# One-hots of an expert-weight stage: from two engines to three

## The reference

```python
s = jnp.einsum('nhpd,hpkd->nhpk', q, subkeys)          # q = x_n @ w_q
sv, si = lax.top_k(s, 16)                              # best 16 of 128 keys, twice
cs, cp = lax.top_k(sums of all pairs, 16)              # best 16 of 256 pairs
e = the chosen experts' numbers;  g = softmax(cs)
act = gelu(jnp.einsum('nd,nhkd->nhk', xt, u_tab[e]))
out = jnp.einsum('nhk,nhkd->nd', g * act, v_tab[e])
```

## Time and profile before

| what | value |
|---|---|
| time, median of 3 runs | 2606.37 us (2605.88 to 2607.01) |
| the profiled execution, its time | 2604.28 us |
| its span, first to last instruction | 2602.4 us |
| TensorE, VectorE, ScalarE, GpSimd busy | 92%, 48%, 44%, 31% of the span |
| mean granted TensorE clock | 0.968 of full speed |
| weights and other data read | 338.65 MB, 131 GB/s over the span |

### The profile page before, as it was taken

One profiled execution on the slowest core, in us unless ns is written; L12 is line 12 of the kernel. 1 busy time (PEld: TensorE's weight loads), 2 busy tenths in 40 slices (PEclk: granted clock), 3 DMA queues, 4 the chain that ended last, 5 costly groups with the idle time before them and its releaser, 6 DMA issues.

```text
span 2602.4 us, 47827 instructions
## 1 busy us (share of the span) xinstructions
PE 2392.1 (92%) x16250; PEld 2219.0 (85%) x16250; DVE 1259.4 (48%) x3541; ACT 1142.8 (44%) x2431; POOL 802.9 (31%) x608
## 2 busy tenths in 40 slices
PE   7989999998669999998899989999999668999998
PEld 5789999998559999996674479999999657999997
DVE  5229980002995555553152124992000896555555
ACT  3345444454444444442252235444454444444443
POOL 0067988775000000000000036988878000000000
PEclk9999999999889999998999899999999988999999
DMA  3343444443004444443224433444444002444443
GB/s 137 124 154 121 155 158 164 161 161 113 1 1 161 162 168 163 167 163 129 71 82 134 142 135 133 155 154 158 162 162 161 25 1 83 168 162 168 161 168 108
DMA packets 107490, 341.93 MB, mean 131 GB/s; under 512 B 12466, under 2 KB 30610, under 8 KB 106514
## 3 DMA queue, kind: packets, MB, share of 16 engines
q1 hardware_dynamic: 103968, 333.76, 37.1%
q10 hardware_dynamic: 3442, 7.19, 0.8%
HBM read 338.65 MB, written 1.66 MB: 131 GB/s over the span
## 4 chain that ended last, share of the span: by engine, by line
PE 42%; DVE 7%; POOL 2%; issue 2%; ACT 1%; ACTq 0%; POOLq 0%; DVEq 0%
PE ps L468 16%; PE ps L397 5%; PE ps L399 5%; PE ps L398 5%; DVE ohj L1062 3%; PE ps L371 2%; POOL lo L1293 2%; PE ps L593 2%; DVE HB L1069 2%; PE ps L618 1%; PE ps L522 1%; DVE ohi L1061 1%; PE ps L565 1%; PE ps L546 1%; PE ps L547 1%
## 5 line engine op out<-in xcount | busy, mean ns | idle before, releaser
L1293 POOL TENSOR_TENSOR lo<-raw,hi 128x512 fp32r<-128x512 f32 x576 | 798.4, 1394 | 525.7 <-ACT hi L685 525.2
L685 ACT ACTIVATE hi<-raw 128x512 fp32r<-128x512 f32 x1088 | 655.1, 625 | 483.2 <-PE ps L399 483.1
L397 PE MATMUL ps<-XH,hi 128*128 128x288 f32 x2304 | 687.2, 298 | 35.7 <-POOL lo L1293 18.7
L398 PE MATMUL ps<-XL,hi 128*128 128x288 f32 x2304 | 681.6, 296 | 0.0
L399 PE MATMUL ps<-XH,lo 128*128 128x288 f32 x2304 | 679.3, 295 | 0.0
L468 PE MATMUL ps<-WH,hi 128*128 128x288 f32 x2048 | 605.4, 296 | 6.5 <-DVE lo L1088 6.5
L468 PE MATMUL ps<-WH,lo 128*128 128x288 f32 x2048 | 606.0, 296 | 0.0
L468 PE MATMUL ps<-WL,hi 128*128 128x288 f32 x2048 | 605.4, 296 | 0.0
L397 PEld LDWEIGHTS ps<-XH,hi 128*128 128x128 f32 x2304 | 433.5, 188 | 42.1 <-POOL lo L1293 24.4
L399 PEld LDWEIGHTS ps<-XH,lo 128*128 128x128 f32 x2304 | 435.8, 189 | 0.0
L398 PEld LDWEIGHTS ps<-XL,hi 128*128 128x128 f32 x2304 | 434.6, 189 | 0.1
(11 more groups left out here) (218 smaller groups left out, 1900.8 us busy)
## 6 DMA issues: line engine op xcount, KB each, us to landing
raw<-in_stream SPq DMA_DIRECT2D x592, 512.0 KB, 3.2
pkeys<-in_pool SPq DMA_DIRECT2D x64, 192.0 KB, 3.1
plat<-in_pool SPq DMA_DIRECT2D x64, 128.0 KB, 2.2
SK<-in_sk ACTq DMA_DIRECT2D x2, 1024.0 KB, 6.8
X<-in_x SPq DMA_DIRECT2D x1, 1152.0 KB, 5.6
out_y<-X SPq DMA_DIRECT2D x1, 1152.0 KB, 4.2
wg<-in_wg ACTq DMA_DIRECT2D x1, 1024.0 KB, 10.5
wuk<-in_wuk ACTq DMA_DIRECT2D x1, 1024.0 KB
```

The source lines that it names most:

```text
L397: pe.matmul(ps[s][:, 0:TOK], h, XH[:, c, :], start=c == 0, stop=False)
L398: pe.matmul(ps[s][:, 0:TOK], h, XL[:, c, :], start=False, stop=False)
L685: act.activation(hi[k % 4][:], raw[s][:, half * HALF:(half + 1) * HALF], ACT.Copy)\
L1293: pool.tensor_tensor(lo[k % 4][:], raw[k // 2][:, half], hi[k % 4][:].bitcast(F32), ALU.subtract)\
```

## The change

In the expert-weight stage GpSimd makes all `ohi`, by the same compare that VectorE used. The `ohj` alternate: VectorE makes those of even groups, as before, and ScalarE those of odd groups, as relu(GT - GT (column - JT)²): four squares into a buffer of their own (`DJ`, two of them), then four relus, each with a per-partition scale (`NGT`, the negated weight) and bias (`GT`). The squares of an odd group are made one odd group ahead. VectorE's even one-hots run four groups ahead of the product instead of two. VectorE prepares two small arrays (`NJT`, `NGT`) in place of one (`NIT`). GpSimd waits for the weights and for the last matmul of the first half before it starts; TensorE waits for one semaphore of each one-hot.

```diff
-        NIT = at("NIT", HL + 2048, [P, TOK])
+        NJT = at("NJT", HL + 2048, [P, TOK])
+        NGT = at("NGT", HL + 2048 + TOK, [P, TOK])
+        DJ = [at(f"DJ{b}", HL + 2048 + 2 * TOK + 512 * b, [P, 4, P]) for b in range(2)]
@@ tensor
                 for g in range(NGRP):
                     n = NGRP * l + g
-                    pe.wait_ge(oh_ready, n + 1)
-                    if g % 2:
-                        pe.wait_ge(ohi_ready, NACT * l + g // 2 + 1)
-
+                    pe.wait_ge(ohi_ready, n + 1)
+                    pe.wait_ge((ohj_dve, ohj_act)[g % 2], NACT * l + g // 2 + 1)
@@ scalar
-                act.wait_ge(nit_ready, l + 1)
+                act.wait_ge(ng_ready, l + 1)
+
+                def square_of_difference(k):
+                    if k >= 2:
+                        act.wait_ge(ohj_act, NACT * l + k - 1)
+                    for t in range(4):
+                        n = 4 * (2 * k + 1) + t
+                        ins = act.activation(DJ[k % 2][:, t, :], iota[:], ACT.Square, bias=NJT[:, n:n + 1])
+                    ins.then_inc(dif_sq, 1)
+
+                square_of_difference(0)
                 for k in range(NACT):
                     g = 2 * k + 1
+                    if k + 1 < NACT:
+                        square_of_difference(k + 1)
                     if NGRP * l + g >= 4:
                         act.wait_ge(g_done, NGRP * l + g - 3)
+                    act.wait_ge(dif_sq, NACT * l + k + 1)
                     for t in range(4):
                         n = 4 * g + t
-                        ins = act.activation(ohi[g % 4][:, t, :], iota[:], ACT.Square, bias=NIT[:, n:n + 1])
-                    ins.then_inc(dif_sq, 1)
-                    act.wait_ge(dif_sq, NACT * l + k + 1)
-                    act.activation(ohi[g % 4][:], ohi[g % 4][:], ACT.Relu, scale=-1.0, bias=1.0).then_inc(ohi_ready, 1)
+                        ins = act.activation(ohj[g % 4][:, t, :], DJ[k % 2][:, t, :], ACT.Relu,
+                                             scale=NGT[:, n:n + 1], bias=GT[:, n:n + 1])
+                    ins.then_inc(ohj_act, 1)
@@ vector
-                dve.tensor_scalar(NIT[:], IT[:], -1.0, None, ALU.mult).then_inc(nit_ready, 1)
+                dve.tensor_scalar(NJT[:], JT[:], -1.0, None, ALU.mult)
+                dve.tensor_scalar(NGT[:], GT[:], -1.0, None, ALU.mult).then_inc(ng_ready, 1)
 
                 def g_onehot(g):
                     if NGRP * l + g >= 4:
                         dve.wait_ge(g_done, NGRP * l + g - 3)
                     for t in range(4):
                         n = 4 * g + t
-                        if g % 2 == 0:
-                            dve.tensor_scalar(ohi[g % 4][:, t, :], iota[:], IT[:, n:n + 1], None, ALU.is_equal)
                         ins = dve.tensor_scalar(ohj[g % 4][:, t, :], iota[:], JT[:, n:n + 1], GT[:, n:n + 1],
                                                 ALU.is_equal, ALU.mult)
-                    ins.then_inc(oh_ready, 1)
+                    ins.then_inc(ohj_dve, 1)
...
                 g_onehot(0)
-                g_onehot(1)
+                g_onehot(2)
                 for g in range(NGRP):
-                    if g + 2 < NGRP:
-                        g_onehot(g + 2)
+                    if g % 2 == 0 and g + 4 < NGRP:
+                        g_onehot(g + 4)
                     g_apply(g)
@@ gpsimd
+                pool.wait_ge(gt_ready, l + 1)
+                pool.wait_ge(mm_done, SPLIT[f"u{l}"] + 2 * P)
+                for g in range(NGRP):
+                    if NGRP * l + g >= 4:
+                        pool.wait_ge(g_done, NGRP * l + g - 3)
+                    for t in range(4):
+                        n = 4 * g + t
+                        ins = pool.tensor_scalar(ohi[g % 4][:, t, :], iota[:], IT[:, n:n + 1], None, ALU.is_equal)
+                    ins.then_inc(ohi_ready, 1)
```

More of the change, by code:

```diff
@@ L250, in build @@
             "topk_done", "tr_done", "ex_ready", "bs_done", "gt_ready"))
-        nit_ready, dif_sq, ohi_ready, oh_ready, g_done, g_used = map(sem, (
-            "nit_ready", "dif_sq", "ohi_ready", "oh_ready", "g_done", "g_used"))
+        ng_ready, dif_sq, ohi_ready, ohj_act, ohj_dve, g_done, g_used = map(sem, (
+            "ng_ready", "dif_sq", "ohi_ready", "ohj_act", "ohj_dve", "g_done", "g_used"))
         kr_ready, ct_ready, cnt_done, cn_ready, qr_ready, qr_in = map(sem, (
```

## The result

The changed kernel takes 2655.2 us (2652.81 to 2657.93, 4 runs) beside 2606.69 before: ratio 1.0187, 95% interval 1.0175 to 1.0199. It is slower by 1.9%, against a forecast of 1% faster, and 0.2 us beyond the upper end of the range.

A forecast was written before the change was run, and what follows sets the result against it. VectorE was taken to bound the expert-weight stage at 4.03 us a pair; GpSimd's 3.61 saves 15.1 us in 36 pairs, less 1.2 for the start, 27.8 over two layers. Forecast 2579 us, 1.05% faster; range 2524 to 2655.

The forecast's parts named there:

- The stage, its pace and its bound: Expert-weight stage: VectorE alone bounds it at 4.03 us a pair of token groups, 36 pairs a layer; GpSimd afterwards.
- The loop of four buffers: One-hot buffers: four groups are two pairs, 7.1 us, enough for the longest loop of 4.2.
- its four relus: ScalarE's odd ohj: four relus taken at 1.28 us a pair, between 0.63 and 1.56.
- The start: Start of the stage: group 1 waits for ScalarE's squares and relus, costing 1.2 us a layer.
- the price of GpSimd's one-hot: GpSimd's ohi loop: 0.37 us for each ohi, eight a pair, 2.96 us.
- its own sign of being wrong: GpSimd's ohi loop: the forecast would be wrong if ohi took more than 0.42 us apart.
- The two bounds: GpSimd's ohi price: 0.28 us from copies, 0.48 from the two-input subtraction, each including 0.06 for the operand.
- The rival in which GpSimd becomes the bound and the kernel slower: GpSimd's ohi loop: at 0.48 us each, 2638 us, or 2670 with 0.26 lost per VectorE one-hot; chance 0.32.
- The hindrance: GpSimd's ohi loop: 0.15 us lost to each VectorE one-hot, 0.6 us a pair.
- VectorE's wait of half a GpSimd instruction: VectorE's even ohj: four waits a pair of 0 to 0.37 us, bringing VectorE to some 3.0 us a pair.
- The exclusion and the copy's rate: One-hots: VectorE and GpSimd exclude each other for whole instructions; rival with GpSimd's one-hot at a copy's price, 2540, chance 0.16.
- TensorE's clock: TensorE's matmuls: low clock for 0.24 of the stage, needing 3.78 us a pair there, adding 0.05 us.

The follow-up runs named there:

- Runs 6 and 7: Changed kernel with GpSimd comparing only the first 32 (6) or 64 (7) of each ohi's 128 columns: 2518.2 and 2568.06 us.
- run 3: Changed kernel with GpSimd comparing with a constant in place of the per-partition operand: 2632.55 us.
- Runs 1 and 2: Changed kernel with VectorE's one-hots taken out after the first two of a layer (1), or doubled into spare buffers (2): 2651.06 and 2651.71 us.
- run 8: Changed kernel without its GpSimd part: VectorE makes all ohi, ScalarE the odd ohj; 2588.98 us, ratio 0.9932.
- run 9: Changed kernel with half of ohi on GpSimd: VectorE makes both one-hots of even groups, GpSimd odd ohi, ScalarE odd ohj; 2536.96 us, ratio 0.9736.
- run 10: Half of ohi on GpSimd, with VectorE's four ohi of an even group made by one 512-column compare: 2528.34 us, ratio 0.9699.

## Why the prediction was wrong

**The stage, its pace and its bound** were read rightly: a stage of VectorE alone, 4.03 us a pair, and GpSimd as the engine that sets the pace after. The loop of four buffers held. ScalarE's squares took 1.28 and were never the bound; its four relus took 1.63 to 1.65, just above the upper end of 1.56, without effect. The start cost 1.1 us a layer against 1.2, but the agreement is luck. The sum had TensorE wait there for ScalarE's relus, and that wait is 0.5 us. VectorE's first product is late because the `ohj` of group 4 now stand ahead of it, and they wait for TensorE's first group:

```profile
636.12 1.38 DVE L1073 TENSOR_SCALAR ohj<-iota,JT,GT 128x128 f32<-128x128 f32 x4 [1.51 <-PE ps L457]
637.41 0.67 DVE L1080 TENSOR_TENSOR HB<-HB,ps 128x512 f32<-128x512 f32 x1
```

**The step that failed is the price of GpSimd's one-hot.** The prediction took 0.37 us from bounds of 0.28 and 0.48; it is 0.577 alone, past the 0.42 that it named as its own sign of being wrong. The two bounds shared one assumption that the trace did not carry: the base of 0.13 us, taken from the spacing of small copies, was put under both ends. Runs 6 and 7 show a fixed part of 0.25 to 0.28; how much of it is the operand's (0.04 to 0.09 at 128 columns, run 3) was not tried. The slope of the upper bound, 2.27 ns a column from the two-input subtraction, was nearly right (2.4 to 2.6). With a base of 0.25 to 0.28 in place of 0.13, the same subtraction would have given 0.51 to 0.53, and 0.57 to 0.59 with the operand's 0.06. The rival in which GpSimd becomes the bound and the kernel slower named the right place, and 2655 lies between its two prices, 2638 and 2670, but with another division of them: 0.48 and 0.15 to 0.26 lost to each VectorE one-hot, where 0.577 and 0.014 were measured.

**The hindrance was over-sized.** The sum held 0.15 us lost to GpSimd for each VectorE one-hot, 0.6 a pair. The one row behind it gave 0.05, and there GpSimd began 0.03 us after the cast, not at the cast's end, so it gave no reason to go up to 0.15. Runs 1 and 2 bound it in the changed kernel: 8 x (0.584 - 0.577) = 0.06 a pair, 0.014 for each. It is some 0.04 for each in runs 6 and 7, so it is no constant, but for these tensor_scalars nowhere 0.15. VectorE's wait of half a GpSimd instruction, 0.18 us, is 0.04: its four `ohj` hold it for 1.09 us from 644.42 to 645.51, for 1.17 on average, where they held 1.02; the longest wait of one is 0.23. Their mean length, 384 ns where it was 329, must not be read as this wait, since it is as great in run 8 with GpSimd idle, where the four hold VectorE for 1.02 as before (681.62 to 682.64):

```profile
L1073 DVE TENSOR_SCALAR ohj<-iota,JT,GT 128x128 f32<-128x128 f32 x108 | 31.4, 392 | 0.0
```

The two errors partly cancel: the price was 8 x 0.207 = 1.66 us a pair too low, the hindrance 0.54 too high. With the measured prices the step reads 8 x 0.577 + 0.06 = 4.68, the 4.63 to 4.68 seen; 36 x 0.65 + 1.1 = 24.5 a layer and 49 us in all, against 48.5.

**The exclusion and the copy's rate.** The Trainium skill (SBUF — State Buffer, "Who interferes with whom") says that a VectorE operation in a two-port mode and a GpSimd operation exclude each other for a whole instruction. The cast behind a subtraction agrees, and the prediction carried this over to the one-hots. There it is not seen: VectorE's `ohj` waits for 0.23 us at most, and the `ohi` of run 9, which has one per-partition operand as the rows that the prediction compared it with the earlier trace rows, for 0.13 at most, beside GpSimd instructions of 0.58. The measurement decides; that these one-hots run in such a mode was argued from their rate and is not shown. A hold of nearly a whole instruction does come back in run 10, with GpSimd as the one that waits. The Trainium skill (GPSIMD Engine Reference, "Engine selection") also says that one-input operations run on GpSimd at roughly line rate. That holds for the copy, 0.24 us for 128 columns, and not for the tensor_scalar, 0.58.

**TensorE's clock** did not matter in the changed kernel. The granted clock is 0.73, so about (1 - 0.73) / 0.5 = 0.54 of the stage is low, where the prediction had 0.24; but at low clock a group takes 2.08 us, under the 2.32 of GpSimd:

```profile
680.30 2.08 PE L457 MATMUL ps<-ohj,ohi 128*128 128x128 f32 x8 [0.23 <-POOL ohi L1315]
```

Nothing of the loss stays open: the pace of the stage accounts for it. Why the fixed part is 0.25 to 0.28 us, and why the short tensor_scalars hinder each other so little when a cast waited for a whole subtraction, was not tried.

## What to carry to other kernels

An operation that the trace of an engine does not show can cost more than every bound drawn from its neighbours there; before a whole share is moved to GpSimd, measure one instruction of exactly that kind and shape, or move a part of the work small enough that the worst neighbour still fits. Divide work among engines by measured prices: here 0.58 us on GpSimd against 0.20 on VectorE. With ScalarE's part in all three, the kernel is 0.7% faster than before with no `ohi` on GpSimd, 2.6% faster with half of them, and 1.9% slower with all. Many small instructions on GpSimd pay its fixed part each time.

## What the runs showed of the hardware that was not expected

- On GpSimd a tensor_scalar of 128 fp32 columns takes 0.58 us from start to start, compare or subtraction alike; 2.4 to 2.6 ns a column and a fixed 0.25 to 0.28 us. Of the 0.58, a per-partition operand makes 0.04 to 0.09. A copy of the same size takes 0.24.
- VectorE's two-input compare of 512 columns is hardly held up itself (699 ns beside 684) and holds up the one GpSimd instruction that it meets (1.10 us from start to start instead of 0.58).
- TensorE's granted clock in the stage went with its waits: 0.73 in the changed kernel, where TensorE waits some 1.15 us ahead of each group at full clock, 0.88 before, with 1.25 and 0.47 in turn; 0.99 in run 8 at 3.78 us a pair; in run 7, with waits of 0.5 to 0.7 us, it is 1.00, and so in run 9, with 1.05 ahead of two groups. Run 7, the stretch and TensorE:

```profile
640.00:740.00 100.00, 67.18 (x464) 56.13 (x464) 69.28 (x175) 86.60 (x239) 100.00 (x233) 1.00 0.00 1
```

```profile
681.52 1.16 PE L457 MATMUL ps<-ohj,ohi 128*128 128x128 f32 x8 [0.49 <-POOL ohi L1317]
683.35 1.16 PE L457 MATMUL ps<-ohj,ohi 128*128 128x128 f32 x8 [0.67 <-POOL ohi L1317]
```

Faster one-hots thus also kept the matmuls at full clock, 1.16 us a group here, and a share of low clock taken over from the kernel before, as the prediction's 0.24, is too high for a faster stage and too low for a slower one.
